# Down projections in parts of 8, 8 and 6 tiles, and three tables of the next stage computed elsewhere

## The reference, cut to what matters

```python
def _swiglu(x, w_gate, w_up, w_down):
    return (jax.nn.silu(x @ w_gate) * (x @ w_up)) @ w_down

def rope_tables(positions):           # rotary angles, for the mixer after FFN 3
    inv_freq = ROPE_BASE ** (-jnp.arange(0, QK_ROPE_DIM, 2, dtype=jnp.float32) / QK_ROPE_DIM)
    ang = positions.astype(jnp.float32)[..., None] * inv_freq
    return jnp.cos(ang), jnp.sin(ang)

    # odd mixer, after FFN 4: the decay rates
    log_a = -LRU_C * r.astype(jnp.float32) * jax.nn.softplus(-lam.astype(jnp.float32))
    ...
x = x + 0.5 * swiglu(rms_norm(x)) ...   # FFN 0 to 3; FFN 4 and 5 without the 0.5
```

## Time and profile before

| | before |
|---|---|
| median of 3 runs | 3107.25 us (3105.91 to 3107.46) |
| profiled execution | 3107.77 us |
| its span | 3106.5 us |
| granted TensorE clock, mean | 0.997 |
| TensorE busy | 3081.8 us, 99% |
| VectorE busy | 2172.2 us, 70% |
| ScalarE busy | 1625.5 us, 52% |
| GpSimd busy | 1650.9 us, 53% |
| weight units by DMA | 588, 512 KB each, 3.3 us to landing |

### The profile page before, as it was taken

How to read it: one execution, slowest core, us unless ns; L and a number is a source line. 1 busy time by engine, 2 the same in 40 slices (tenths; PEclk the granted TensorE clock), 3 DMA queues, 4 the chain that set the end, 5 groups by cost and what they waited for, 6 DMA issues and landing times. The chain is left out here.

```text
span 3106.5 us, 52754 instructions
## 1 busy us (share of the span) xinstructions
PE 3081.8 (99%) x20424; PEld 2828.5 (91%) x20424; DVE 2172.2 (70%) x2975; ACT 1625.5 (52%) x2567; POOL 1650.9 (53%) x994
## 2 busy tenths in 40 slices
PE   9999999999999999999999999999999999999999
PEld 8999888999989998888999877889999888889998
DVE  8776467877668774577877678558785786478773
ACT  6555433555556554335555455555554585455553
POOL 5676433677657675434767433226675112257664
PEclk9999999999999999999999999999999999999999
DMA  3323322232322332322323232322233223322232
GB/s 142 112 103 122 120 75 75 102 110 109 123 88 104 109 118 101 113 82 82 110 109 110 92 96 82 122 90 108 100 119 110 91 96 122 108 91 107 109 117 74
DMA packets 93320, 322.61 MB, mean 104 GB/s; under 512 B 10512, under 2 KB 14992, under 8 KB 93072
## 3 DMA queue, kind: packets, MB, share of 16 engines
q1 hardware_dynamic: 87680, 312.07, 28.5%
q10 hardware_dynamic: 5392, 7.17, 0.7%
HBM read 316.05 MB, written 2.10 MB: 102 GB/s over the span
## 5 line engine op out<-in xcount | busy, mean ns | idle before, releaser
L3122 POOL TENSOR_TENSOR wlo<-raws,whi 128x1024 fp32r<-128x1024 f32 x369 | 892.0, 2421 | 1127.9 <-ACT whi L1218 876.4
L1218 ACT ACTIVATE whi<-raws 128x1024 fp32r<-128x1024 f32 x422 | 441.4, 1052 | 159.5 <-PE bank L505 57.2
L3130 POOL TENSOR_TENSOR f_s<-f_s,R 128x512 f32<-128x512 f32 x132 | 172.3, 1306 | 200.6 <-ACT f_s L1305 199.2
L640 PE MATMUL bank<-gxh,whi 128*128 128x256 f32 x1064 | 268.8, 283 | 1.2 <-ACT acc L1361 1.2
L641 PE MATMUL bank<-gxl,whi 128*128 128x256 f32 x1064 | 268.6, 283 | 0.0
L2215 DVE TENSOR_TENSOR wlo<-banks,whi 128x1024 fp32r<-128x1024 f32 (+1 forms) x166 | 196.9, 1186 | 68.9 <-ACT whi L1332 68.9
L640 PE MATMUL bank<-f_th,f_sh 128*128 128x256 f32 x944 | 237.7, 284 | 5.5 <-DVE bank L2229 5.5
L641 PE MATMUL bank<-f_tl,f_sh 128*128 128x256 f32 x944 | 237.3, 284 | 0.0
L640 PE MATMUL bank<-f_th,whi 128*128 128x256 f32 x944 | 236.7, 283 | 0.0
L641 PE MATMUL bank<-f_tl,whi 128*128 128x256 f32 x944 | 236.7, 283 | 0.0
L501 PE MATMUL bank<-gxh,whi 128*128 128x512 f32 x584 | 229.9, 394 | 1.4 <-DVE gxl L2157 1.4
(11 more groups left out here) (597 smaller groups left out, 9197.0 us busy)
## 6 DMA issues: line engine op xcount, KB each, us to landing
raws<-stream SPq DMA_DIRECT2D x588, 512.0 KB, 3.3
xa_mem<-memT ACTq DMA_DIRECT2D x2, 1024.0 KB, 6.4
m_dk<-decay ACTq DMA_DIRECT2D x2, 514.0 KB, 4.6
x<-xT ACTq DMA_DIRECT2D x4, 256.0 KB, 5.3
x<-xT SPq DMA_DIRECT2D x4, 256.0 KB, 6.7
outT<-x SPq DMA_DIRECT2D x2, 512.0 KB, 3.0
m_ct<-cos ACTq DMA_DIRECT2D x2, 256.0 KB, 2.6
m_sn<-sin ACTq DMA_DIRECT2D x2, 256.0 KB, 2.9
```

The costliest lines, as they stand in the source:

```text
L640: pe.matmul(out, seq(hi, k, P), moving[k][0], start=first and k == 0, stop=False, skip_group_check=n != 1)
L1218: act.activation(M.whi[r][:, :], M.raw[r][:, :], ACT.Copy).then_inc(*S.tick("hi", u))
L3122: pool.tensor_tensor(M.wlo[r][:, :], M.raw[r][:, :], M.whi[r][:, :].bitcast(F32), ALU.subtract).then_inc(*S.tick("lo", u))
L3130: pool.tensor_tensor(T["s"][:, :], T["s"][:, :], M.R[:, :], ALU.mult).then_inc(*S.tick("silu_scaled", f, m))
```

## The change

The down projection is cut in parts of 8, 8 and 6 tiles instead of 8, 6 and 8: part 1 has 8 tiles in the scheme with seven products, the plain part 2 has 6, and its units are loaded and split with 768 columns instead of 1024. `PAIRED` becomes 16; the hidden copy of tile 16 is made one step later, since its place is read until the third product of the last down step. The first three plain units leave out one tile instead of two. The rotary angles are made in three pieces: piece 0 in the last step ahead of `gate(20)`, piece 1 after it, piece 2 after the last `c22`. The DMA of the positions stands ahead of the split of the second last unit on ScalarE. The sign is given to the sine as its scale, and L2136 goes. The exponential and `decay_rates` stand ahead of the residual of FFN 4.

```diff
-F_PARTS = ((0, 8), (8, 14), (14, 22))
-F_RUNS = ((0, 9), (9, 15), (15, 22))
+F_PARTS = ((0, 8), (8, 16), (16, 22))
+F_RUNS = ((0, 9), (9, 17), (17, 22))
...
+LAST = {U["down", f, 2, m] for f in range(6) for m in range(KD)}
+
+
+def unit_cols(u):
+
+    return (F_PARTS[2][1] - F_PARTS[2][0]) * P if u in LAST else UNIT
...
-        name, k = ("odd", (k + 3) % 4) if k < 4 else ("tur0", k - 4)
+        name, k = ("odd", k) if k < 4 else ("tur0", k - 4)
...
-            part(("down", f, 2, m), banks[m][:, :], pairs, range(0, 6), True, False, arrive if m == 0 else None)
+            part(("down", f, 2, m), banks[m][:, :], pairs, range(0, len(ks) - 1), True, False, arrive if m == 0 else None)
...
-            part(("down", f, 2, m), banks[m][:, :], pairs, range(6, KD), False, True, arrive if m == 0 else None)
+            part(("down", f, 2, m), banks[m][:, :], pairs, range(len(ks) - 1, len(ks)), False, True, arrive if m == 0 else None)
...
-        act.activation(M.whi[r][:, :], M.raw[r][:, :], ACT.Copy).then_inc(*S.tick("hi", u))
+        cols = unit_cols(u)
+        act.activation(M.whi[r][:, 0:cols], M.raw[r][:, 0:cols], ACT.Copy).then_inc(*S.tick("hi", u))
...
-            if i == M3_STAGE - 1 and m == 2:
-                act.wait_ge(*S.at("lam", "ready"))
-                act.activation(M.m3["lt"][:, 0:8], M.m3["lt"][:, 0:8], ACT.Exp, scale=-1.0).then_inc(*S.tick("lam_exp"))
...
-                    act.activation(M.m2[name][:, :], M.m2[name][:, :], ACT.Sin).then_inc(*S.tick("sin", name))
+                    act.activation(M.m2[name][:, :], M.m2[name][:, :], ACT.Sin,
+                                   scale=M.rc("sign") if name == "rsin" else 1.0).then_inc(*S.tick("sin", name))
...
+            if after is None and i == M2_STAGE - 1:
+                act.wait_ge(*S.at("seven", f, s - 1, 4))
+                act.dma_start(M.m2["rsin"][:, :].bitcast(I32), T_in["pos"]).then_inc(*S.tick("pos2", by=16))
             if after is None:
                 split_hi(U["down", f, 2, 1])
...
-            if before[0] == "tile":
+            if before[0] == "tile" and before[1] != PAIRED:
                 hidden_hi(before[1])
...
+            if SEQS[f][s] == ("tile", PAIRED + 1):
+                act.wait_ge(*S.at("seven", f, s - 1, 3))
+                hidden_hi(PAIRED)
...
         hidden_hi(KF - 1)
+        if i == M3_STAGE - 1:
+            act.wait_ge(*S.at("lam", "ready"))
+            act.activation(M.m3["lt"][:, 0:8], M.m3["lt"][:, 0:8], ACT.Exp, scale=-1.0).then_inc(*S.tick("lam_exp"))
...
-            if i == M3_STAGE - 1 and m == 3:
-                decay_rates()
             if i == M3_STAGE - 1 and m == 4:
                 reset_positions()
-            if i == M2_STAGE - 1 and m == 4:
-                dve.wait_ge(*S.at("sin", "rsin"))
-                dve.tensor_scalar(M.m2["rsin"][:, :], M.m2["rsin"][:, :], M.rc("sign"), None, ALU.mult).then_inc(
-                    *S.tick("rope_table"))
...
+            if not after and i == M2_STAGE - 1:
+                rope_angles(0)
             if before[0] == "tile":
                 gate(before[1])
             else:
                 second_row(s - 1)
+            if not after and i == M2_STAGE - 1:
+                rope_angles(1)
...
-            if not after and i == M2_STAGE - 1:
-                rope_angles()
...
         c22(len(SEQS[f]) - 1)
+        if i == M2_STAGE - 1:
+            rope_angles(2)
         gate(KF - 1)
         hidden(KF - 1)
+        if i == M3_STAGE - 1:
+            decay_rates()
         residual(i, lambda m: ("down", f, 2, m), F_SCALE[f])
...
-        sp.dma_start(M.raw[r][:, :], T_in["stream"][u]).then_inc(*S.tick(f"loaded{r}", u, by=16))
+        cols = unit_cols(u)
+        sp.dma_start(M.raw[r][:, 0:cols], T_in["stream"][u][:, 0:cols]).then_inc(*S.tick(f"loaded{r}", u, by=16))
```

More of the change, by code:

```diff
@@ L203 @@
     "m1_tensor": "hvar vdone kturn kv1 score1 inner gturn gmix",
-    "m2_vector": "acc2 angle rope_table Rn c rk rk_s rk_c rk_turned cadd kv_rstd cn q_rstd latent pads pooled ub win "
+    "m2_vector": "acc2 angle Rn c rk rk_s rk_c rk_turned cadd kv_rstd cn q_rstd latent pads pooled ub win "
                  "knope_odd pool_in pool_lo rot_a rot_b rot_q x_scaled",
@@ L601, in last_tile @@
             b = next_bank("xs", 11, KD - 1, half)
-            for k in range(KD):
+            for k in range(len(pairs)):
                 for t in pairs[k]:
@@ L607, in last_tile @@
             pe.wait_ge(*S.at(*low_part(u)))
-            for k in range(KD):
-                mm = pe.matmul(b[:, 0:HALF], seq(lo, k, P), of_half(pairs[k][0], half), start=False, stop=k == KD - 1)
+            for k in range(len(pairs)):
+                mm = pe.matmul(b[:, 0:HALF], seq(lo, k, P), of_half(pairs[k][0], half), start=False,
+                               stop=k == len(pairs) - 1)
             mm.then_inc(*S.tick("last_half", half))
@@ L1377, in step @@
                 snap(5, s)
-            if after is None and i == M2_STAGE - 1:
-                act.wait_ge(*S.at("seven", f, s - 1, 4))
-                act.dma_start(M.m2["rsin"][:, :].bitcast(I32), T_in["pos"]).then_inc(*S.tick("pos2", by=16))
             if after is not None:
@@ L2011, in scale_x, with rope_angles @@
             *S.tick("x_scaled", m))
-    def rope_angles():
+    def rope_angles(piece):
         T = M.m2
@@ L2019, in rope_angles @@
         p3 = TWO_PI - p1 - p2
[L2020 to L2032, removed]
-        dve.tensor_scalar(angle, angle, float(np.pi / 2), None, ALU.add).then_inc(*S.tick("angle", 7))
-        dve.wait_ge(*S.at("angle", 7))
@@ L2035, in rope_angles @@
-        dve.tensor_scalar(whole, angle, float(np.pi), -TWO_PI, ALU.is_gt, ALU.mult).then_inc(*S.tick("angle", 8))
-        dve.wait_ge(*S.at("angle", 8))
-        dve.tensor_tensor(angle, angle, whole, ALU.add).then_inc(*S.tick("angle", 9))
-        dve.wait_ge(*S.at("angle", 9))
-        dve.tensor_scalar(angle, angle, 3.141592, -3.141592, ALU.min, ALU.max).then_inc(*S.tick("angle", "rcos"))
+        if piece == 0:
+            dve.wait_ge(*S.at("pos2"))
+            dve.tensor_copy(angle, T["rsin"][:, :].bitcast(I32)).then_inc(*S.tick("angle", 0))
+            dve.wait_ge(*S.at("angle", 0))
+            dve.tensor_scalar(angle, angle, M.rc("freq"), None, ALU.mult).then_inc(*S.tick("angle", 1))
+            dve.wait_ge(*S.at("angle", 1))
+            dve.tensor_scalar(whole, angle, 1.0 / TWO_PI, 12582912.0, ALU.mult, ALU.add).then_inc(*S.tick("angle", 2))
+            dve.wait_ge(*S.at("angle", 2))
+            dve.tensor_scalar(whole, whole, -12582912.0, None, ALU.add).then_inc(*S.tick("angle", 3))
+        elif piece == 1:
+            for n, part in enumerate((p1, p2, p3)):
+                dve.wait_ge(*S.at("angle", 3 + n))
+                dve.scalar_tensor_tensor(angle, whole, -part, angle, ALU.mult, ALU.add).then_inc(*S.tick("angle", 4 + n))
+            dve.wait_ge(*S.at("angle", 6))
+            dve.tensor_scalar(rsin, angle, 3.141592, -3.141592, ALU.min, ALU.max).then_inc(*S.tick("angle", "rsin"))
+        else:
+            dve.tensor_scalar(angle, angle, float(np.pi / 2), None, ALU.add).then_inc(*S.tick("angle", 7))
+            dve.wait_ge(*S.at("angle", 7))
+            dve.tensor_scalar(whole, angle, float(np.pi), -TWO_PI, ALU.is_gt, ALU.mult).then_inc(*S.tick("angle", 8))
+            dve.wait_ge(*S.at("angle", 8))
+            dve.tensor_tensor(angle, angle, whole, ALU.add).then_inc(*S.tick("angle", 9))
+            dve.wait_ge(*S.at("angle", 9))
+            dve.tensor_scalar(angle, angle, 3.141592, -3.141592, ALU.min, ALU.max).then_inc(*S.tick("angle", "rcos"))
@@ L3121, in lo @@
             return
-        pool.tensor_tensor(M.wlo[r][:, :], M.raw[r][:, :], M.whi[r][:, :].bitcast(F32), ALU.subtract).then_inc(
-            *S.tick("lo", u))
+        cols = unit_cols(u)
+        pool.tensor_tensor(M.wlo[r][:, 0:cols], M.raw[r][:, 0:cols], M.whi[r][:, 0:cols].bitcast(F32),
+                           ALU.subtract).then_inc(*S.tick("lo", u))
     def ffn(f):
@@ L3197, in ffn @@
                 lo(second)
-            if before[0] == "tile":
+            if item == ("tile", PAIRED + 1):
+                hidden_lo(PAIRED)
+            if before[0] == "tile" and before[1] != PAIRED:
                 hidden_lo(before[1])
@@ L3282, in tail_units @@
         if c == 2:
-            out.append(m_tiles(tiles[ks].reshape(UNIT, -1)))
+            rows = np.zeros((KD, *tiles.shape[1:]), w.dtype)
+            rows[0:b - a] = tiles[ks]
+            out.append(m_tiles(rows.reshape(UNIT, -1)))
             continue
```

3 lines of the change are left out of this document (2 added, 1 removed).

## The result

| | before | after |
|---|---|---|
| median | 3106.88 us (3105.46 to 3107.89, 19 runs) | 3111.52 us (3109.31 to 3113.1, 19 runs) |
| ratio to before | | 1.0014 [1.0008, 1.0021] |
| profiled execution, its span | 3107.77, 3106.5 us | 3109.31, 3108.1 us |
| mean granted clock of that execution | 0.997 | 0.999 |

The change costs 0.14%, 4.6 us: under the 0.2% bound of the prediction, but its interval does not reach down to no change. The forecast was a median of 3107.5, so 4.0 us are missing in it.

A forecast was written before the change was run, and what follows sets the result against it. TensorE, busy nearly throughout, was taken as the bound. Gains of -18.5 us and new stalls of +18.7 us gave net +0.2 on the profiled 3107.77: forecast 3108, median 3107.5, range 3097 to 3117 us.

The forecast's parts named there:

- the second rival: New idle stretches at the angles, FFN 4 and ends of FFN 1 and 3 halve the clock; two or more falls 3114 to 3119, chance 0.24.
- two sums of 18 us: Whole kernel: gains of -18.5 us against new stalls of +18.7 us, net +0.2 us.
- Matmuls, short stalls: All six FFNs: fewer matmul columns, -4.9 us; six waits of about 1.1 us in the second down part go, -6.2 us.
- Residual of FFN 1: End of FFN 1: VectorE's chain of 31.2 us outlasts TensorE's 24.9, a new stall of +6.3 us.
- Residual of FFN 3: End of FFN 3: VectorE's chain, without the sign multiplication, takes 28.7 us against 24.9, a stall of +3.8 us.
- Residual of FFN 4: End of FFN 4: decay rates moved ahead make the first x 3.4 us late; stall +4.3 us, net +3.2.
- Angles: End of FFN 3: the 5.5 us stall and 1.9 us of slow clock go; new waits of 3.6 and 1.2 us come.
- The term for product 7: Last down step of FFN 3: TensorE waits for snapshot 6 behind the positions' DMA, 3.0 to 4.9 us, taken 3.6.
- The term for the fifth tile: End of FFN 3: piece 1 delays hidden 20, whose low part TensorE wants; 0.9 to 2.5 us, taken 1.2.
- FFN 2 and FFN 0 into a mixer: Residuals of FFN 0 and 2: the mixer takes its last gx tile late, so only +0.3 us each for the first split.
- The signs: Listed trace marks: no old waits, new gx waits, VectorE idle over 7 us, late first x; wrong if half clock in several residuals.
- the rivals that are slower: Two or more falls to half clock, 3114 to 3119, chance 0.24; or the six short stalls stay, 3114, chance 0.04.

The follow-up runs named there:

- e4: The changed kernel unaltered, run once more beside its parts on one chip; 3111.97 us, ratio 1.0014.
- e1: Kernel before with only the parts of 8, 8 and 6 tiles and the 768 column units, angles and decay rates as before; 3116.01 us, ratio 1.0028.
- e6: Changed kernel with FFN 1's addition of squares for residual tiles 0 to 6 on 1 column instead of 512; 3107.66 us, ratio to before 1.0004.
- e7: Changed kernel with GpSimd's subtraction for the last part's units on 1024 columns again instead of 768; 3115.89 us, ratio 1.0029.
- e9: Changed kernel with angle piece 0 after the last c22, piece 1 between gate 21 and hidden 21, piece 2 after hidden 21; 3111.09 us, ratio 1.0015.
- e2: Kernel before with only the angles in three pieces, the earlier DMA and the sign in the sine; 3103.35 us, ratio 0.9987.
- e5: Changed kernel with angle pieces 0 and 1 after the last c22, piece 2 between gate 21 and hidden 21; 3111.26 us, ratio 1.0014.

## Why the prediction was right, and where it was short

The time lies in the range and within 0.2% of before, but the sum was 4 us too low. The largest thing it lacked was the mechanism of the second rival. Its closeness is in part luck: +0.2 was the difference of two sums of 18 us, and terms that came out too high hid some of what was missing.

- *Matmuls, short stalls.* FFN 0, which has nothing else, gives -1.5 us as predicted (-0.8 - 1.0 + 0.3; e4 -1.2), and the waits for line 2234's successor are absent. e1 shows that the parts alone remove them. Right.
- *Residual of FFN 1.* Chain predicted 31.2 us, measured 31.1. Stall predicted 6.3; the waits in the trace are 0.5 + 1.1 + 0.2 for hi and 1.2 + 2.9 for gx, 6.0. e6 shows by shortening it that this chain sets the time, e7 that the relief by the shorter GpSimd operations is real (0.75 us here, for 1.2).
- *Residual of FFN 3.* Chain predicted 28.7, measured 28.7 (1767.81 to 1796.54); stall predicted 3.8, measured 1.85 + 2.07 = 3.9.
- *Residual of FFN 4.* From hidden 21's end to the first x 7.4 us were predicted, and they are 7.5 (2412.95 to 2420.48). The stall was predicted as 4.3 (3.2 more than before) and is 4.0. Its place was wrong: it doesn't gather at the last gx tile, but is one wait for the hi part of the fifth unit, whose split on ScalarE stands behind the late x. So it was one stretch of 4 us, not several short ones, and the clock fell behind it. The rival had named that place; the sum had no half clock for it.
- *Angles.* That the stall is moved was right. The term for product 7 was mis-sized: 3.6 predicted (3.0 to 4.9), 1.9 measured. The DMA landed 3.0 us after its issue, where I had taken 3.4 to 5.3, and from landing to the end of snapshot 6 were 3.4 us, not 3.9. The term for the fifth tile was 1.2 (0.9 to 2.5) and is 1.8, as three operations of piece 1 took 3.11 us. Together 3.7 instead of 4.8.
- *FFN 2 and FFN 0 into a mixer*: +0.3 each was taken for the first split; FFN 0 alone can be told apart, and its row agrees.
- *Half clock.* This is the step that failed. The sum had no half clock behind the new waits and left it to a rival, which asked for two falls to take place with a chance of 0.24. By the windows e4, a run near the median, has two that matter, 2.4 us at the start of FFN 2 and 1.7 in FFN 4. Their 4.1 us are as much as the median is above the forecast (4.0), but that they agree so well is chance: the other terms (angles, FFN 1, 3 and 4) were together 1.6 us too high, so 1.6 us more lie in e4's rows, 0.2 to 0.6 in each, that none of these terms accounts for. The rival's own time (3114 to 3119) was too high all the same, because it put 2.9 us on each fall and came on top of an angle term that was 1.1 too large. That the lost time is a half clock rests on the windows; no run here changed the clock alone.
- *Rows of before that spoke for the rival.* Against it the prediction held that no fall follows the waits of about 1 us. It did not use the end of the program, where before's own trace falls to 0.50 behind a wait of 1.69 us (the line of before under e4). A wait of 3 us could not be taken as safe by that.
- *The signs.* Present are: no waits of line 2234 and none of 5.5 us, the first x of FFN 4 late by over 3 us, and units of 18 matmuls in 4.08 us. VectorE's idle time for the positions was just short of its mark (6.91 for over 7 us), the wait ahead of product 7 well short (1.9 for 3 to 5), and at mixer 3 no wait for gx shows. One sign of being wrong came true: the clock reads half behind the residuals of FFN 1 and in that of FFN 4, and in e4 at the end of FFN 3 too. (The chances of the rivals that are slower add to 0.28, where the prediction's last list has 0.27.)

What stays open: why the same waits are followed by 3.4 us at half clock in one execution, by 6.8 in another and by none in a third (e6), and why the clock behind the residual of FFN 3 fell in e9 and not in after. Nor is the missing 1.6 us placed. It also wasn't tried whether a reordered ScalarE, with the fifth unit's split ahead of the first x, would keep the short parts in FFN 4.

## What to carry to other kernels

Shortening the bound engine's work in a stretch is worth nothing beyond the point at which another engine's chain through the same stretch ends: add up that chain first, from its first operation to the one that the next stage waits for, and decide stage by stage, not for all six at once. Here the same cut gained in FFN 0, where the next stage comes late to its inputs, and lost in the three stages where it doesn't; made only in the first kind, with the angles spread, it turned +4.6 us into -11.7 (the angles and the decay rates have a share in that). A step moved out of the way costs its wait wherever the next consumer has no slack, and a new wait of 2 to 4 us should be priced with the slow clock that may stand behind it, not left to a rival.

## What the runs showed of the hardware

- *The clock behind a stall.* The length of a stall did not decide it here. After's profiled execution kept 1.00 behind stalls of 1.6 to 2.1 us and fell behind those of 2.9 and 4.0; but before and e4 fell behind a wait of 1.7, e9 behind one of 2.1 and e2 behind one of 2.3, while e6 kept 1.00 behind the stall of 2.9 behind which after fell. e4, with the same instructions as after, worked at half clock for 4.80 us at the start of FFN 2, where after has 3.14 at 0.54. The runs of the changed kernel spread over 3.8 us, the fastest at a mean clock of 0.999 and the slowest at 0.996; before's spread over 2.4. The Trainium skill (TensorE: Matmul & The Clock Gate, "What's actually happening") names the same two levels, 1.2 and 2.4 GHz, and the windows at 0.50 and 1.00 agree.
- *VectorE beside GpSimd.* Operations with a single input are stretched too: `TENSOR_SCALAR` of 128x512 takes 0.43 us alone and 1.95 to 1.96 beside a GpSimd operation (e5, e9), and the cast of the positions 0.45 in after and 0.99 in e9. The Trainium skill (SBUF - State Buffer, "Who interferes with whom") says this of `tensor_scalar` and `cast` in modes that take both port pairs, beside the two-input rule that the prediction used; the trace agrees with both. The misses of e5 and e9 were in part operations of that kind, priced as if alone (1.96 of the 4.6 us of piece 2 in e5, 1.95 of the 5.1 of piece 1 in e9), though the earlier trace rows already has one at 2.61 us.
